# Taps of a depthwise convolution moved beside an attention, its norm interleaved with a compression

## What is computed

```python
h = rms_norm(x, norm_g)
z = h @ w_in                                   # split by columns
o_a = fox_attention(fq, fk, fv, ff + fox_b) * silu(f_gate)      # 4 heads, decayed by cumsum(log_sigmoid)
o_b = conformer_conv(glu_in, ...) * silu(c_gate)
o_c = nsa_attention(...) * silu(n_gate)        # 8 heads; uses compressed keys and values
x = x + concat([o_a, o_b, o_c]) @ w_out

def conformer_conv(u, conv_w, conv_b, ln_g, ln_b, w_pw):
    a, b = split(u, 2)
    y = a * sigmoid(b)
    y = depthwise_conv(y, conv_w, taps=31) + conv_b      # 256 channels
    yn = layer_norm(y) * ln_g + ln_b
    return silu(yn) @ w_pw

def compress(x, pe, w1, w2):                   # for keys and for values
    blk = x[:, cmp_idx] + pe                   # 31 blocks of 32 tokens, stride 16, 2 groups
    return gelu(blk.reshape(..., 32 * 64) @ w1) @ w2
```

## Time and profile before

| what | value |
|---|---|
| median of 3 runs | 3899.86 us |
| profiled execution, its own time | 3894.39 us |
| its span | 3892.6 us |
| TensorE busy (PE) | 3504.1 us, 90% |
| weight loads (PEld) | 2889.2 us, 74% |
| VectorE busy (DVE) | 2094.9 us, 54% |
| ScalarE busy (ACT) | 1451.1 us, 37% |
| GpSimd busy (POOL) | 408.5 us, 10% |
| mean granted clock of TensorE | 0.94 |

### The profile page before, as it was taken

One profiled execution on the slowest core, in us unless ns is written; L12 is line 12 of the kernel. 1 busy time (PEld: TensorE's weight loads), 2 busy tenths in 40 slices (PEclk: granted clock), 3 DMA queues, 4 the chain that ended last, 5 costly groups with the idle time before them and its releaser, 6 DMA issues. The chain is left out here.

```text
span 3892.6 us, 48517 instructions
## 1 busy us (share of the span) xinstructions
PE 3504.1 (90%) x17756; PEld 2889.2 (74%) x17756; DVE 2094.9 (54%) x4076; ACT 1451.1 (37%) x2809; POOL 408.5 (10%) x322
## 2 busy tenths in 40 slices
PE   7968889868889999898989999999998889999998
PEld 5857867757668788777777888777887778777886
DVE  3564544466547886455664333358784545753333
ACT  3303333123334454343434322345453443434222
POOL 0000000000002222000111111112221000202111
PEclk9978899878899999999999999999999899999999
DMA  5633027440043322513433333343233432433332
GB/s 142 186 71 96 9 71 214 98 106 10 27 121 101 98 82 82 140 57 92 118 88 105 97 93 93 92 140 89 79 94 81 109 93 76 126 104 88 92 97 82
DMA packets 570478, 373.52 MB, mean 96 GB/s; under 512 B 77020, under 2 KB 500956, under 8 KB 569980
## 3 DMA queue, kind: packets, MB, share of 16 engines
q10 hardware_dynamic: 416768, 209.74, 19.7%
q1 hardware_dynamic: 153468, 160.59, 14.7%
HBM read 310.69 MB, written 59.57 MB: 95 GB/s over the span
## 5 line engine op out<-in xcount | busy, mean ns | idle before, releaser
L790 PE MATMUL bank<-h,w_hi 128*128 128x512 f32 (+2 forms) x2240 | 963.4, 430 | 101.5 <-DVE w_low L777 55.7
L791 PE MATMUL bank<-h,w_hi 128*128 128x512 f32 (+2 forms) x2240 | 905.6, 404 | 0.0
L792 PE MATMUL bank<-h,w_low 128*128 128x512 f32 (+2 forms) x2240 | 904.1, 404 | 0.0
L771 ACT CAST w_hi<-w 128x1024 fp32r<-128x1024 f32 (+2 forms) x456 | 434.3, 952 | 848.5 <-PE bank L792 679.7
L777 DVE TENSOR_TENSOR w_low<-w,w_hi 128x1024 fp32r<-128x1024 f32 (+2 forms) x456 | 508.2, 1114 | 368.7 <-ACT w_hi L771 357.0
L790 PEld LDWEIGHTS bank<-h,w_hi 128*128 128x128 f32 (+2 forms) x2240 | 432.6, 193 | 225.5 <-issue 70.3
L792 PEld LDWEIGHTS bank<-h,w_low 128*128 128x128 f32 (+2 forms) x2240 | 431.2, 193 | 108.3
L791 PEld LDWEIGHTS bank<-h,w_hi 128*128 128x128 f32 (+2 forms) x2240 | 432.9, 193 | 101.0 <-issue 13.5
L791 PE MATMUL bank<-yT_low,w_hi 128*128 128x512 f32 x768 | 308.8, 402 | 0.0
L1461 ACT ACTIVATE prob<-bank,softmax_stat 128x512 f32<-128x512 f32 (+3 forms) x256 | 144.9, 567 | 330.3 <-DVE softmax_stat L1495 222.2
L355 PE MATMUL bank<-v_tok,prob_T 128*128 128x64 f32 (+1 forms) x1376 | 195.1, 276 | 7.5 <-DVE y_tok L2138 3.8
(11 more groups left out here) (411 smaller groups left out, 5803.5 us busy)
## 6 DMA issues: line engine op xcount, KB each, us to landing
w<-in_w_in ACTq DMA_DIRECT2D x144, 512.0 KB, 4.3
w<-in_w_mlp ACTq DMA_DIRECT2D x128, 512.0 KB, 4.1
w<-in_w_gate ACTq DMA_DIRECT2D x64, 512.0 KB, 4.2
z<-z_tile SPq DMA_DIRECT2D x110, 256.0 KB, 4.2
w<-in_w_branch ACTq DMA_DIRECT2D x64, 256.0 KB, 2.9
z_hi<-row_part_high SPq DMA_DIRECT2D x54, 256.0 KB, 2.0
z<-z_tile_low SPq DMA_DIRECT2D x54, 256.0 KB, 2.3
k_hi<-z_hi SPq DMA_DIRECT2D x36, 256.0 KB, 6.9
```

What stands on the lines that cost most here:

```text
L771: self.a.copy(self.wh[s][:, 0:d, 0:n], self.w[s][:, 0:d, 0:n]).then_inc(self.w_high.sem, 1)
L790: self.t.matmul(bank[0:n, :], wh, high, start=j == 0, stop=False)
L791: self.t.matmul(bank[0:n, :], wh, low, start=False, stop=False)
L792: return self.t.matmul(bank[0:n, :], wl, high, start=False, stop=j == self.depth(i) - 1)
```

## The change

The GLU and the taps leave `ConvAndCompress` for `Fox`, as side generators `taps_act` and `taps_dve` that go on by one part at each attention step. SyncE asks for the GLU rows and taps once the stream is two units past the last GLU row. Two taps (four VectorE steps) follow each attention step. The accumulator and the GLU operands use parts of `yT` that were free; `glu_padded`, the taps and the parameters live across both stages. For this the projection's order changes: first pair's rows, the four GLU rows, second pair's rows, then the queries. `Fox` yields 7 and 4 pieces instead of 5 and 3 ahead of its first pair. `ConvAndCompress` runs the norm and the compression together: one step of the norm to three of the compression, 1.1 pieces after each; the norm's banks are now 4 and 5, the ones of the gate. SyncE waits once, for the row `nvc`, and then issues all loads.

```diff
-ORDER1, PLACE1 = sequence(C1, LAST1, (("ff",), ("fq", "fk", "fv", "fg"), ("nq",), ("glu",), ("cg",), ("nkc",), ("nvc",), ("nks",), ("nkw",),
-                                      ("nvs",), ("nvw",), ("ng",)))
+FOX_ROWS = ("fq", "fk", "fv", "fg")
+ORDER1, PLACE1 = sequence(C1, LAST1, ((("ff",),), (FOX_ROWS, 0), (("glu",),), (FOX_ROWS, 1), (("nq",),), (("cg",),), (("nkc",),), (("nvc",),),
+                                      (("nks",),), (("nkw",),), (("nvs",),), (("nvw",),), (("ng",),)))
...
+    def taps_sp(self):
+
+        stream, s, A, l, row = self.stream, self.s, self.A, self.l, PLACE1["glu", 3]
+        if self.glu_asked or stream.halts < stream.begins[row + 2]:
+            return
+        self.glu_asked = True
+        stream.wait_stored(s, row)
...
+    def taps_dve(self):
+        self.v.memset(self.glu[:, :, 0:TAPS - 1], 0.0).then_inc(self.cleared.sem, 1)
+        while not self.glu_asked:
+            yield
+        yield
+        yield
+        yield
+        for j in range(2):
+            x = self.opened[:, j, :]
+            self.v.wait_ge(*self.b_tanh(j))
+            self.v.tensor_scalar(x, x, 0.5, 0.5, ALU.mult, ALU.add).then_inc(self.b_opened.sem, 1)
+            self.v.wait_ge(*self.b_opened(j))
+            self.v.wait_ge(*self.a_in(0))
+            self.v.tensor_tensor(self.glu[:, j, TAPS - 1:], x, self.za[:, j, :], ALU.mult).then_inc(self.glu_made.sem, 1)
+        yield
+        self.v.wait_ge(*self.cleared(0))
+        self.v.wait_ge(*self.taps_in(0))
+        for w in range(TAPS):
...
+            if w % 2:
+                yield
...
     def pe(self):
         for p in range(2):
-            yield 5.0
+            yield 5.0 if p else 7.0
...
-            yield 3.0
+            yield 3.0 if p else 4.0
...
-            yield from self.attend_dve(p)
+            yield from self.attend_dve(p, taps)
...
     def layer_norm_pe(self):
         ones = self.k.tab("ones")
-        self.t.wait_ge(*self.tapped(TAPS - 1, 1))
-        self.t.wait_ge(*self.kc_sin(1))
-        products(self.t, self.bank[0][:, :], [(ones, self.acc[:, j, :]) for j in range(2)]).then_inc(self.summed.sem, 1)
-        yield 3.0
+        self.t.wait_ge(*self.g_made(0))
+        products(self.t, self.bank[4][:, :], [(ones, self.acc[:, j, :]) for j in range(2)]).then_inc(self.summed.sem, 1)
+        yield
...
+def every(count, part):
+
+    for _ in part:
+        for _ in range(count):
+            yield
...
     def pe(self):
-        yield 5.0
+        yield 4.0
         self.gates_pe()
-        yield 1.0
-        side = self.compress_pe()
-        for w in range(TAPS):
-            if w >= self.TOKENS_AT:
-                next(side, None)
-            yield 0.2
-        yield from self.layer_norm_pe()
+        yield 2.0
+        for _ in together(every(3, self.layer_norm_pe()), self.compress_pe()):
+            yield 1.1
...
     def dve(self):
...
+        yield from together(every(3, self.layer_norm_dve()), self.compress_dve())
```

More of the change, by code:

```diff
@@ L79, in sequence @@
     order = []
-    for names in groups:
+    for names, *some in groups:
         rows = [range(first[name] // P, last[name] + 1) for name in names]
+        if some:
+            rows = [[row[j] for j in some] for row in rows]
         order += [tile for part in zip(*rows, strict=True) for tile in part]
@@ L1548, with __init__ @@
+class Fox(Attention, Taps):
     decayed = True
     score_banks, other_banks, share = 2, ((2, 3), (4, 5)), 1.6
-    def __init__(self, k, l, stream, w1):
+    def __init__(self, k, l, stream, w1, kept):
         super().__init__(k)
         self.l, self.stream, self.w1 = l, stream, w1
+        self.init_taps(kept)
         sb = self.sb
@@ L1664, in act @@
             yield
-            yield from self.attend_act(p)
+            yield from self.attend_act(p, taps)
             yield
     def dve(self):
-        flat = lambda x: x[:, :, :].rearrange("p t n -> p (t n)")
+        flat, taps = lambda x: x[:, :, :].rearrange("p t n -> p (t n)"), self.taps_dve()
         yield
@@ L1728, in conv_sp @@
         z, A, s, l = self.k.z1, self.A, self.s, self.l
[L1729 to L1737 removed]
+        s.dma_start(self.zg[:, :, :], z[C1["cg"]:C1["cg"] + CONV_CH, :].rearrange("(j p) t -> p j t", p=P)).then_inc(self.g_in.sem, 16)
         s.dma_start(self.wp[:, :, :], A["conv_pw"][l].rearrange("(k p) n -> p k n", p=P)).then_inc(self.wp_in.sem, 16)
@@ L1775, in gates_act @@
     def gates_act(self):
-        self.a.wait_ge(*self.b_in(0))
-        for j in range(2):
-            self.a.activation(self.sq[:, j, :], self.zb[:, j, :], ACT.Tanh, scale=0.5).then_inc(self.b_tanh.sem, 1)
         self.a.wait_ge(*self.g_turned(0))
@@ L2052, in act @@
         yield
-        side = self.compress_act()
-        for w in range(TAPS):
-            if w >= self.TOKENS_AT:
-                next(side, None)
-            yield
-        yield from self.layer_norm_act()
+        yield from together(every(3, self.layer_norm_act()), self.compress_act())
     def dve(self):
         yield
-        self.glu_dve()
+        self.gates_dve()
         yield
-        side = self.compress_dve()
-        for w in range(TAPS):
-            if w >= self.TOKENS_AT:
-                next(side, None)
-            self.tap_dve(w)
-            yield
-        yield from self.layer_norm_dve()
+        yield from together(every(3, self.layer_norm_dve()), self.compress_dve())
     def pool(self):
@@ L2074, in pool @@
         yield
-        side = self.compress_pool()
-        for w in range(TAPS):
-            if w >= self.TOKENS_AT:
-                next(side, None)
-            yield
-        for _ in range(4):
-            yield
+        yield from self.compress_pool()
 class Nsa(Attention):
@@ L2350, in layer_one @@
         with ExitStack() as inner:
+            kept = [inner.enter_context(k.nc.sbuf_tensor(f"{name}_{k.stage}", shape, F32)) for name, shape in (
+                ("glu_padded", [P, 2, TAPS - 1 + T]), ("taps", [P, TAPS, 2]), ("conv_params", [P, 3, 2]))]
             w1 = [inner.enter_context(k.nc.sbuf_tensor(f"cmp_w1_{i}_{k.stage}", [P, CMP_LEN // 2, 256], F32)) for i in range(2)]
@@ L2355, in layer_one @@
             stream.until(stream.units[PLACE1["nvc", 0] + 2])
-            Fox(k, l, stream, w1).beside(stream, stream.units[PLACE1["nvc", 0] + 2])
+            Fox(k, l, stream, w1, kept).beside(stream, stream.units[PLACE1["nvc", 0] + 2])
             stream.until(stream.units[PLACE1["ng", 2]])
-            ConvAndCompress(k, l, stream, kcmp, vcmp, table, w1).beside(stream, stream.units[PLACE1["ng", 2]], stream.forms_out)
+            ConvAndCompress(k, l, stream, kcmp, vcmp, table, w1, kept).beside(stream, stream.units[PLACE1["ng", 2]], stream.forms_out)
             stream.forms.close()
```

125 lines of the change are left out of this document (61 added, 64 removed).

## The result

| | before | after |
|---|---|---|
| median, us | 3900.53 (4 runs) | 3846.8 (4 runs, 3843.34 to 3854.77) |
| ratio | | 0.9863, 95% interval 0.9842 to 0.9883 |
| span of the profiled execution, us | 3892.6 | 3847.9 |

The change saves 53.7 us; I had forecast 21. The sign and the range held, the size did not. Three windows of the changed kernel's first layer (columns as in the earlier trace rows): the whole decayed attention, its second pair alone, the stage of convolution and compression.

The account below looks back on a forecast made before the run. TensorE, busy 90% of the span, was taken as the bound, its waits in the stage due to VectorE's in-order queue. Per layer -31 + 20 + 4.5 - 5 + 1 = -10.5, in two layers -21: 3879 us, range 3842 to 3902.

Parts of the forecast that it names:

- The sign and the range: Whole kernel: faster than before, at 0.78; range to hold 8 in 10 from 3842 to 3902 us.
- The stage: Convolution and compression, per layer: 80.5 us after the change, 31 us less than 111.
- the 128 matmuls to take 27.5 us once more: Compression's narrow products: clock falls in the gap ahead, one interleaved piece does not raise it, so 27.5 us again.
- The gap of 4.1 us: Between the sum and the first compression matmul: mean 0.60, subtractions 1.29, blocks 2.00, some 4.1 us with hand-offs.
- the open 2.4 us: Chain from the squares' sum to the pointwise product: 3 pieces cover 4.2 of 6.6 us, 2.4 stay open.
- My list: Stage's terms on TensorE: 48.5 + 4.1 gap + 27.5 narrow products + 2.4 open chain = 82.5 us.
- The 2 us that I took off the list: Stage: the same list for the kernel before gives some 2 us more than measured, so 82.5 became 80.5.
- Rival 1: Compression's narrow products keep the full clock: 13.8 us instead of 27.5, -16.5 per layer, total 3846 us; chance 0.19.
- The second pair: Attention: VectorE's queue of 53.8 us against TensorE's 36.4 gives +17.4, late weight splits +2.6, together +20 per layer.
- Start and first pair: Attention, per layer: start -5 (idle 3 us, clock kept), first pair's end +4.5, tap loads +1.
- The forecast's own range: Total from the bounds of the first pair (-4.5 to +8) and the start (-4 to +4): 3863 to 3896 us.
- Rivals 2 and 3: Tap loads hold up weights, 3892 us, chance 0.15; clock falls and stays down in the second pair, 3911 us, 0.11.

Follow-up runs that it names:

- k_then_v: Changed kernel with the stream piece between the keys' and values' products moved behind both: 3859.9 us, ratio 0.9908.
- fill_all: Changed kernel plus 18 throwaway wide identity matmuls between the first sum and the keys' products: 3829.5 us, ratio 0.9830.
- fill_all_k_then_v: Changed kernel plus the 18 throwaway matmuls, with the values' 64 products directly behind the keys' 64: 3830.9 us, ratio 0.9839.
- half_taps: Changed kernel computing only the first 16 of 31 taps: 3825.8 us, ratio 0.9835; second pair 46.6 us.
- pieces_in_gap: Changed kernel with three stream pieces and the squares' sum between the first sum and the keys' products: 3813.0 us, ratio 0.9794.
- late_behind_blocks: Changed kernel with keys and values ahead of the norm's sum, the last 8 taps back in the stage behind the token blocks: 3831.8 us, ratio 0.9847.
- shared_taps: On the kernel with real pieces in the gap: ScalarE multiplies the last 8 taps, GpSimd adds them, VectorE joins: 3844.5 us, ratio 0.9871.

## Why the prediction was wrong

**The stage** (forecast 80.5, measured 70.6) holds 10.4 of the 17.1 us that each layer is off. The step that failed: "Between the 62-column runs one piece is interleaved; that is not enough to raise it", and with it "the 128 matmuls to take 27.5 us once more". The clock was back 17 us after its fall, at the end of that piece with its two rotation products, and the 128 matmuls took 13.88 + 7.25 = 21.1 us, 6.4 less; k_then_v, without the piece, shows the 27.2 us that I had forecast. The gap of 4.1 us was measured at 4.03, the fall of the clock in it came as described, the open 2.4 us ahead of the pointwise product were 2.42.

The rest of the miss is in the sum. My list ran to 82.5 us, 11.9 above the measured time: 6.4 for the narrow products, 3.3 for other matmul work (45.5 in the list, 63.3 - 21.1 = 42.2 in the window), 1.8 for waits and barriers (9.5 in the list, 71.0 - 63.3 = 7.7 in the window). The clock has a part in the 3.3 too: the list had 6.5 us of pieces at half clock, about 3 were measured. The 2 us that I took off the list made up for part of it, and the 111 us that I started from are 112.1 from barrier to barrier.

Rival 1 was right about the mechanism for the half that had no stop ahead, and fill_all and fill_all_k_then_v show it for all of it; I had taken a block that starts slow as evidence on one that starts fast. That its total, 3846, is nearly the measured 3846.8 is chance: it has the stage at 64 us, 6.6 below the measured one, and the attention of the first layer ended 6.7 us better than it says.

**The second pair** (+20, measured +18.0): VectorE's sum of 53.8 us (its first two terms are 15.8 + 30.8 = 46.6) stands against 51.6 busy in 54.5; the waits came where described, up to 4.42 us. Its reasoning, the longer of two queues plus a little, was right only because this queue is full from end to end; half_taps shows where it breaks.

**Start and first pair** (-5 + 4.5 + 1, measured -1.2 up to the second pair). Three more pieces now stand ahead of that mark, 4.2 us, and four rotation products fewer, some 2 us; the three pieces are missing behind the second pair, where the row of the table is -3.0. I had no term for pieces that move from a phase's end to its start, and priced the start at idle 3 us with the clock kept: it was 4.90, and the clock fell to 0.50. Against it, the first pair's end cost 1.5 + 1.2 us of waits and not 4.5, and the stop at the pair's turn of the kernel before, with its slow clock, did not return, which no term had. That stop was 2.31 us, not the 2.4 of my text:

```profile
152.03 0.50 PE L790 MATMUL bank<-h,w_hi 128*128 128x512 f32 x1 [2.31 <-DVE w_low L777]
```

**The forecast's own range**: its upper end does not follow from the bounds named for it, which reach to 3903 (+8 and +4 us in each of two layers) and not to 3896. Nothing else hangs on it.

**Rivals 2 and 3** did not come: the second pair's clock was 0.90, and TensorE waited for no late load in either pair.

## What to carry to other kernels

Price a stop of TensorE not only by its length: here 4 us of idle time cost 6.6 us more in the narrow matmuls behind it, through which the clock stayed down. Put real work into the gap, where it costs nothing (pieces_in_gap: -14.8 us per stage), before moving anything else. And cost work put beside other work step by step: in half_taps the longer queue counted in each step, and a light step gave nothing back to a heavy one.

## What the runs showed of the hardware

- 128 matmuls of 62 columns with no stop ahead of them held 2.4 GHz for 14.5 us (fill_all_k_then_v). Behind stops of 1.82 to 4.04 us the keys' products fell to 1.2 GHz, at the latest 2.4 us after their start, and stayed there to their end, with the values' behind them up to 27.3 us in all (k_then_v) with TensorE recorded busy all through. One profiled kernel is the exception (late_behind_blocks, stops of 1.84 and 1.89 us, nothing lost). The Trainium skill ("TensorE: Matmul & The Clock Gate", What's actually happening) says that the default is the throttled state and activity releases it; by recorded busy time that does not agree with these 27.3 us at a clock of 0.50.
- GpSimd, adding 128x512 in SBUF in 1578 ns each, stretched VectorE's taps from a mean of 743 to 1049 ns (30 x 0.306 = 9.2 us for 12 additions) and a product of two SBUF operands from 681 to 1149 (shared_taps); the drain, which reads a bank, stayed at 681. The Trainium skill ("SBUF — State Buffer", SBUF: two separate sides) describes a port pair that VectorE, with two SBUF inputs, and GpSimd lock from each other for a whole instruction. The rows agree as to which operations grew; the taps lost 0.77 us for each addition of 1.58.
